# A decoder layer's mixture of experts: the order in which the 32 experts' places are worked

## The reference, cut to what matters

```python
g_sel = jnp.argmax(g_prob, axis=-1)                      # 4 groups
top_w, top_i = lax.top_k(e_prob, TOP_K_EXPERTS)          # 2 of the group's 8 experts
...
h = jax.nn.silu(jnp.einsum('nd,edf->nef', xt, e_gate[sl])) * jnp.einsum('nd,edf->nef', xt, e_up[sl])
h = h * comb[:, g, :, None]                              # zero but for the chosen experts
y = y + jnp.einsum('nef,efd->nd', h, e_down[sl])
```

## Time and profile before

| | us |
|---|---|
| median of 2 runs (770.22 to 770.39) | 770.31 |
| the profiled execution's own time | 771.58 |
| its span, first to last instruction | 769.8 |
| first item's `gate_up` starts | 409.28 |
| last item's second half of `gate_up` starts | 666.91 |

### The profile page before, as it was taken

One profiled execution on the slowest core, in us unless ns is written; L12 is line 12 of the kernel. 1 busy time (PEld: TensorE's weight loads), 2 busy tenths in 40 slices (PEclk: granted clock), 3 DMA queues, 4 the chain that ended last, 5 costly groups with the idle time before them and its releaser, 6 DMA issues.

```text
span 769.8 us, 10052 instructions
## 1 busy us (share of the span) xinstructions
PE 657.2 (85%) x3798; PEld 465.2 (60%) x3798; DVE 341.8 (44%) x791; ACT 181.4 (24%) x346; POOL 217.9 (28%) x179
## 2 busy tenths in 40 slices
PE   4998749999999999799627999999999878861897
PEld 3767628787797787688514555555554344351776
DVE  3389994282283274626761112211121111139933
ACT  4265012422423313510210111111111111151230
POOL 6215301620530410641111333333333221133400
PEclk9959769999999999899867999999999999986899
DMA  6402300220120050066394688999999999655002
GB/s 250 150 1 83 138 0 0 76 117 1 56 109 1 1 219 0 2 242 286 125 405 135 239 316 341 418 417 412 415 415 416 415 417 417 270 203 240 1 27 83
DMA packets 30439, 151.21 MB, mean 196 GB/s; under 512 B 7309, under 2 KB 7565, under 8 KB 16433
## 3 DMA queue, kind: packets, MB, share of 16 engines
q1 hardware_dynamic: 23984, 142.08, 46.7%
q0 software_dynamic: 6400, 8.42, 3.1%
HBM read 148.36 MB, written 14.68 MB: 212 GB/s over the span
## 4 chain that ended last, share of the span: by engine, by line
PE 61%; DVE 18%; DMA 9%; SPq 5%; issue 3%; ACT 2%; POOL 1%; POOLq 0%; DVEq 0%; ACTq 0%
PE bank L1788 13%; PE bank L1497 9%; PE bank L1498 9%; PE bank L1499 9%; DMA slots<-in_w_exp_dram 7%; PE bank L1803 7%; SPq L404 4%; DVE raw L996 3%; PE bank L1577 3%; DVE small L992 3%; DVE res L1081 2%; PE bank L1778 2%; PE bank L1586 2%; PE bank L1598 2%; PE bank L1564 2%
## 5 line engine op out<-in xcount | busy, mean ns | idle before, releaser
L1497 PE MATMUL bank<-w_hi,a_hi 128*128 128x512 f32 (+1 forms) x272 | 105.4, 388 | 9.4 <-DVE w_lo L1463 6.3
L1498 PE MATMUL bank<-w_lo,a_hi 128*128 128x512 f32 (+1 forms) x272 | 103.3, 380 | 0.0
L1499 PE MATMUL bank<-w_hi,a_lo 128*128 128x512 f32 (+1 forms) x272 | 102.9, 378 | 0.0
L1426 DVE COPY rows_x<-bank 128x128 f32<-128x128 f32 x40 | 11.7, 292 | 203.7 <-PE bank L1795 105.8
L608 POOL DMA_INDIRECT pair_dram<-rows_x,row_put x40 | 40.5, 1013 | 173.9 <-ACT rows_x L854 173.9
L1788 PE MATMUL bank<-slots,rows_x 128*64 128x256 f32 x640 | 74.1, 381 | 9.3 <-DMA slots<-in_w_exp_dram 9.3
L1788 PE MATMUL bank<-raw,rows_x 128*64 128x256 f32 x640 | 75.2, 386 | 7.9 <-DMA raw<-in_w_exp_dram 6.3
L1497 PE MATMUL bank<-a_hi,w_hi 128*128 128x512 f32 (+1 forms) x176 | 70.9, 403 | 11.3 <-POOL w_lo L518 9.9
L518 POOL TENSOR_TENSOR w_lo<-raw,w_hi 128x1024 fp32r<-128x1024 f32 x19 | 45.2, 2386 | 122.8 <-ACT w_hi L662 122.7
L1788 PEld LDWEIGHTS bank<-slots,rows_x 128*64 128x64 f32 x640 | 46.1, 137 | 43.4 <-issue 18.9
L1788 PEld LDWEIGHTS bank<-raw,rows_x 128*64 128x64 f32 x640 | 46.6, 139 | 41.6 <-issue 17.2
(11 more groups left out here) (236 smaller groups left out, 959.0 us busy)
## 6 DMA issues: line engine op xcount, KB each, us to landing
raw<-in_w_exp_dram SPq DMA_DIRECT2D x48, 1024.0 KB
slots<-in_w_exp_dram SPq DMA_DIRECT2D x48, 1024.0 KB
raw<-in_w_in_dram SPq DMA_DIRECT2D x19, 512.0 KB, 3.8
raw<-in_w_wide_dram SPq DMA_DIRECT2D x4, 1536.0 KB, 6.7
raw<-in_w_out_dram SPq DMA_DIRECT2D x4, 1024.0 KB, 8.0
raw<-pair_dram SPq DMA_DIRECT2D x4, 1024.0 KB, 7.9
res<-in_xT_dram SPq DMA_DIRECT2D x4, 512.0 KB, 6.1
res<-in_x_dram SPq DMA_DIRECT2D x4, 512.0 KB, 5.3
```

Source lines behind the costliest of these rows:

```text
L1497: t_.matmul(o, lh, rh, start=first, stop=False)
L1498: t_.matmul(o, lh, rl, start=False, stop=False)
L1499: return t_.matmul(o, ll, rh, start=False, stop=last)
```

## The change

The list `ORDER` becomes the places in their own order, 0 to 31. Before, three narrow places are worked ahead of place 7, the last wide one, and others between places 4, 5, 6 and 7; after, the eight wide places (16 items) come first and the 24 narrow ones follow. Since `ITEM`, `LAST` and the load loop are made from `ORDER`, the items, the gathers and scatters and the loads of all engines follow the new order. No instruction is added or taken out.

```diff
-ORDER = [0, 1, 2, 3, 4, 8, 9, 5, 10, 11, 6, 12, 13, 7] + list(range(14, NE))
+ORDER = list(range(NE))
 ITEM = [(n, 2 * r + q if r < WIDES else r + WIDES) for n, r in enumerate(ORDER) for q in range(2 if r < WIDES else 1)]
 ITEMS = len(ITEM)
 LAST = [max(i for i in range(ITEMS) if ITEM[i][0] == n) for n in range(NE)]
```

## The result

The changed kernel takes 780.19 us (779.76 to 780.62) against 770.31: a ratio of 1.0124, interval 1.0099 to 1.0148, or +9.9 us. A second measurement of the same kernel, against more runs of before, gave 1.0156 (1.0127 to 1.0185), +11.3.

A forecast was written before the change was run, and what follows sets the result against it. TensorE bounds the experts' part up to item 29, loads from item 30 to 39; the last landing sets the end. Owed bytes 8.4 plus restart 2.3 make 10.7 us later: 781.0 us for the median, range 776 to 787.

The forecast's parts named there:

- Steps 1 and 2: Loads of turns 9 to 11 asked for 6, 12, 12 us later; q1 carries 9.45 MB, not 12.68, by 502.6: 3.23 owed.
- Step 3: Behind 502.6 us, the owed 3.23 MB at q1's 0.385 MB per us cost 8.4 us.
- Step 4: At 502.6 us the load queue is empty; restarting it costs 2.3 us, as at 466.3.
- step 7: Gathers and scatters: same 80 at the same item numbers; charged nothing, with 1.5 us either way.
- Step 5: From turn 11 on, loads are issued at least as fast as served (6.03 against some 8 us), so later asking costs nothing.
- the rival of the shallow queue: Behind 502.6 us one load under way at a time, 10.1 us each: 792 or 821; chance 0.09 with the upper bound.
- Step 6: TensorE first waits for weights at item 25 or 26, 561 to 568 us instead of 591.78; the end is unaffected.
- Step 8: After the last item the tail stays the same, from the landing of the last rows to the end.
- The owed bytes were not made good: Rival, no change: loads behind 502.6 run near 7.75 us, +1.5 us, 771.8; chance 0.08 for anything up to +6.
- TensorE's clock: Rival: clock falls to the lower level in the longer stall, over 14 waiting items, +55 us, 836; chance 0.02.
- the low bound of 771.8: Loads behind 502.6 us taking the lowest time, 7.75 us each, so the end comes 1.5 us later than before.

The follow-up runs named there:

- The lighter loads: Two kernels, before's order and the changed order, leaving out 15 of 16 parts of the down weights of turns 4 to 31: 750.58 and 749.99 us.
- the held loads: Kernel before with its order of work untouched, only the load loop's waits taken from the changed kernel: 780.87 us, ratio 1.0119.

## Why the prediction was right, point by point

**The bound.** Right: the end is set by when the last load lands. The lighter loads took the difference between the orders away altogether, and the held loads gave most of it, 9.15 of 10.71 us, without moving an item.

**Steps 1 and 2, later asking and owed bytes.** Right. The issues are 12.07 us apart, and the three cycles carried 9.44 MB (9.45 forecast) where before had 12.68, so 3.24 MB were owed for the 3.23 forecast.

**Step 3, their price.** 66.68 MB lay behind the third cycle against 63.27, 3.41 MB more. At 0.385 MB per us that is 8.9 for 8.4 us. Only 3.24 of them are owed bytes: the other 0.17 are loads that had got further at the moment of reading (76.12 MB since item 9's issue, for 75.95 before).

**Step 4, the restart.** From 499.8 to 674.9 are 175.1 us; 66.68 MB at 0.385 take 173.2. The rest, 1.9 us, is what is left for the restart, for 2.3. In the held kernel, which moved no item, the same sum leaves less: 66.51 MB take 172.8 of its 173.5 us, and 0.7 us are left; with the bytes of all queues (70.74 and 71.14 MB, at before's 411 GB/s) it is 1.4 us there and 2.0 in the changed kernel. So the restart was priced too high.

**How close the sum is.** The sum of 10.7 met the measured 10.71, and that is partly luck. It was a price for the late asking alone, and that measured 9.15 with the items in before's order; the moved items, charged at nothing in step 7, added 1.56. The two errors cancel.

**Step 5, the queue behind it.** Right: from 511.8 on 412 GB/s moved to the end, so the rival of the shallow queue did not come about, nor its price.

**Step 6, the first wait.** Right. Forecast for item 25 or 26 at 561 to 568 us; it is item 25 at 560.83, which in the time of the trace before would be 563.6.

**Step 7, the rows.** The one term that was mis-sized without showing in the sum: charged at nothing with 1.5 us either way. Against the held loads the moved items cost 1.56 us, just past that bound, 0.6 of it counted as row bytes.

**Step 8, the tail.** Right. From the last second half to the end of the span are 103.2 us in the changed kernel (674.82 to 778.0) and 102.9 before (666.91 to 769.8).

**The rivals.** The owed bytes were not made good: the waiting items came 8.14 us apart in the middle of the stretch (575.82 to 583.96) and 7.74 at its end, as before. TensorE's clock stayed at 1.00, the upper level (2.4 GHz), in the longer stalled stretch too: from 558 to 675 us it waited 29 times for weights, 0.4 to 1.2 us each, and was busy 92.8 of 117 us. The rule of the Trainium skill, TensorE: Matmul & The Clock Gate, section HAM oscillation, where a matmul loop fell back to half clock at each of its longer waits for DMA, did not bite with these short waits.

**Two readings of the prediction that do not hold.** The 5.25 us of the first item are not its time at half clock: the granted clock of 0.71 in that stretch is a mean over both levels. And the low end of the range, 776, is about half way from the forecast of 781.0 to the low bound of 771.8, not a third. Neither enters the sum.

**The absolute time.** 781.0 forecast, 780.19 measured, 782.23 in the second measurement. The span of the first trace is 778.0 for the 780.5 forecast, since its item 2 starts 2.8 us earlier. The scatter comes from the work ahead of the experts: in the nine traces item 2 starts between 419.15 and 422.43 us.

## What to carry to other kernels

Where a ring of buffers feeds a part that is bound by its loads, an order of the work is worth mainly the moments at which it leaves the queue empty: count the bytes that the new order cannot have asked for by the time the queue runs full, divide by the full rate, and add a restart (0.7 to 2 us here, by how it is counted). What the moved items change beside that was 1.6 us here, and only a kernel with the late asking and no moved item could tell the two apart. Asking earlier gains at most the idle and slow time that it takes away, not the time by which it asks earlier. Long items belong neither where the queue is still empty nor at the end, where they become a backlog of their own.

## What the runs showed of the hardware that was not expected

A busy share near 1.00 need not mean the full rate. Just after a restart the DMA engines showed a share of 1.00 and moved 375 GB/s (502.0 to 511.8 us in the changed kernel); with loads queued behind one another it was 1.02 and 416. The same is seen before from 468 to 477, with 0.98 to 0.99 and 369 to 371. The share is modelled, and why the rate was lower there is not shown. So the bytes are the measure: here the share hid about a tenth of the rate.
